# A two-layer decoder trunk on one core: x issued right behind the constants, the first layer's rows rounded out of PSUM, the rotation angles computed later

## The reference

```python
h = rms_norm(x, ln_mix_g[i])            # x * rsqrt(mean(x*x) + 1e-6) * g
proj = h @ w_in[i]                      # split into gates, conv, q_lat, kv_lat, k_rope, glu
q  = (rms_norm(q_lat,  q_norm_g)  @ w_uq)
kv = (rms_norm(kv_lat, kv_norm_g) @ w_ukv)
k_rope = apply_rope(k_rope_raw, cos, sin)   # cos, sin of positions * inv_freq
```

## Time and profile before

| | us |
|---|---|
| median of 3 runs | 1143.59 |
| lowest and highest of them | 1140.56, 1143.98 |
| span of the profiled execution | 1142.2 |
| TensorE busy in the span | 1090.8 |
| VectorE, ScalarE, GpSimd busy | 649.1, 356.2, 134.8 |

### The profile page before, as it was taken

How to read it: one execution, slowest core, us unless ns; L and a number is a source line. 1 busy time by engine, 2 the same in 40 slices (tenths; PEclk the granted TensorE clock), 3 DMA queues, 4 the chain that set the end, 5 groups by cost and what they waited for, 6 DMA issues and landing times. The chain is left out here.

```text
span 1142.2 us, 21367 instructions
## 1 busy us (share of the span) xinstructions
PE 1090.8 (95%) x8168; PEld 859.8 (75%) x8168; DVE 649.1 (57%) x1353; ACT 356.2 (31%) x600; POOL 134.8 (12%) x163
## 2 busy tenths in 40 slices
PE   5999999999899999999989999999999999999996
PEld 5988998998765555554889799999887555555566
DVE  6687997455543333333777879975437333333356
ACT  4355442233331111111663454423334111111143
POOL 0121320011000001000002032101101000000000
PEclk9999999999999999999999999999999999999998
DMA  7558974546279999999454778663644999999962
GB/s 205 131 158 257 304 228 147 151 145 204 111 275 407 416 417 417 418 418 385 135 148 135 224 248 240 200 184 113 179 134 168 400 417 417 417 418 418 417 219 95
DMA packets 202981, 300.39 MB, mean 263 GB/s; under 512 B 14000, under 2 KB 166544, under 8 KB 186512
## 3 DMA queue, kind: packets, MB, share of 16 engines
q1 hardware_dynamic: 202896, 299.28, 73.9%
HBM read 298.21 MB, written 1.05 MB: 262 GB/s over the span
## 5 line engine op out<-in xcount | busy, mean ns | idle before, releaser
L738 PE MATMUL ps<-h_pair,wsplit 128*128 128x256 f32 x2880 | 370.6, 289 | 16.0 <-DVE h_pair L1845 7.4
L738 PEld LDWEIGHTS ps<-h_pair,wsplit 128*128 128x128 f32 x2880 | 356.9, 194 | 24.3 <-issue 15.1
L1836 DVE TENSOR_TENSOR wsplit<-ring,wsplit 128x1024 fp32r<-128x1024 f32 x136 | 167.4, 1235 | 64.6 <-ACT wsplit L1295 60.7
L1295 ACT ACTIVATE wsplit<-ring 128x1024 fp32r<-128x1024 f32 x136 | 141.5, 1055 | 198.6 <-PE ps L738 116.8
L738 PE MATMUL ps<-gu_ring,hT 128*64 128x256 f32 x896 | 107.6, 383 | 3.1 <-DMA gu_ring<-in_w_exp_up_dram 3.1
L1958 DVE SCALAR_TENSOR_TENSOR work<-work,convT 128x256 f32<-128x256 f32 x240 | 104.7, 508 | 0.0
L1522 ACT ACTIVATE prow<-ps 128x128 f32<-128x128 f32 x64 | 17.7, 277 | 277.9 <-PE ps L738 277.9
L738 PEld LDWEIGHTS ps<-gu_ring,hT 128*64 128x64 f32 x896 | 61.7, 137 | 47.7 <-issue 14.0
L2249 DVE TENSOR_TENSOR hT_r<-ps,hT_r 128x512 fp32r<-128x512 f32 x64 | 44.3, 692 | 88.2 <-ACT hT_r L1295 88.2
L2234 DVE TENSOR_TENSOR prow<-prow,ps 128x128 f32<-128x128 f32 x64 | 18.4, 288 | 131.7 <-ACT prow L1522 131.7
L738 PE MATMUL ps<-work,ring 128*128 128x256 f32 x384 | 85.7, 379 | 0.0
(11 more groups left out here) (213 smaller groups left out, 1149.6 us busy)
## 6 DMA issues: line engine op xcount, KB each, us to landing
ring<-in_w_in_dram SPq DMA_DIRECT2D x104, 512.0 KB, 4.6
down_ring<-in_w_exp_down_dram SPq DMA_DIRECT2D x40, 1024.0 KB, 19.1
gu_ring<-in_w_exp_gate_dram SPq DMA_DIRECT2D x28, 1024.0 KB, 14.8
gu_ring<-in_w_exp_up_dram SPq DMA_DIRECT2D x28, 1024.0 KB, 17.0
lent_down<-in_w_exp_down_dram SPq DMA_DIRECT2D x24, 1024.0 KB, 19.6
gu_last<-in_w_exp_gate_dram SPq DMA_DIRECT2D x12, 1024.0 KB, 14.0
gu_last<-in_w_exp_up_dram SPq DMA_DIRECT2D x12, 1024.0 KB, 16.2
ring<-in_w_exp_gate_dram SPq DMA_DIRECT2D x12, 1024.0 KB, 14.9
```

The lines of the kernel that those rows point to most:

```text
L738: return nc.tensor.matmul(o, lhsT, rhs, start=first, stop=last)
L1295: return nc.scalar.activation(o, i, ACT.Copy)
L1836: TT(tile_split[:, m, 1, :, :], tile_of(name, m), tile_split[:, m, 0, :, :].bitcast(F32), ALU.subtract).then_inc(tile_low, 1)
```

## The change

- SyncE issues the constants, then x, then chunks `kv` and `q0` (four halves), then the positions, `w_kr` and the rest. The first layer's nine vector transfers are issued from ScalarE's queue. The positions now count on `kr_loaded`.
- ScalarE first runs a Sigmoid on one column, which loads that table.
- TensorE waits for constants and vectors, turns `vrow`, then x, then `crow`.
- ScalarE makes `h_high` straight from the PSUM banks, with g as scale (`first_high`, two operations a bank), and VectorE `h_low` from the same banks (`first_low`). The copies to `xT` (`first_x`) are all VectorE's and come after. Squares of x come after those copies. `hT`, needed only for the rotary key, is made by ScalarE as in the second layer.
- The first layer's kv is opened by `project_open` too. q0 waits until x is copied, since it uses one of its banks.
- The angles' first four steps come after q0 has been taken out of PSUM, the other six after the diagonal of kv. Sine and cosine come after the weights of q2, ahead of those of gg0.

```diff
@@ SyncE
-            sp.dma_start(ang[:, 0, :].bitcast(I32), positions[0].partition_broadcast(P)).then_inc(init_loaded, 16)
             sp.dma_start(cst[:, :], consts[:, :]).then_inc(init_loaded, 16)
+            sp.dma_start(xin, x[0].rearrange("(t q) d -> q t d", q=P)).then_inc(x_loaded, 16)
...
-            load_vectors(0)
-            sp.dma_start(xin, x[0].rearrange("(t q) d -> q t d", q=P)).then_inc(x_loaded, 16)
             for l in range(DEPTH):
                 load_chunk(l, CHUNKS[0])
+                load_chunk(l, CHUNKS[1])
                 if l == 0:
+                    sp.dma_start(ang[:, 0, :].bitcast(I32), positions[0].partition_broadcast(P)).then_inc(kr_loaded, 16)
                     load_rope_key(l)
@@ TensorE
-            pe.wait_ge(init_loaded, 32)
+            pe.wait_ge(init_loaded, 16)
+            pe.wait_ge(small_loaded, 16 * SMALL)
+            tr(ps[:, 7, 0:VROWS], vrow[:, :], VROWS).then_inc(vec_tr, 1)
             pe.wait_ge(x_loaded, 16)
...
+                project_open()
                 if l == 0:
-                    project_split("kv", "mix")
-                else:
-                    project_open()
+                    pe.wait_ge(x_in, 4)
                 project_split("q0", between=stat_of_x)
@@ ScalarE
+            load_vectors(act, 0)
+            act.wait_ge(const_set, 3)
+            nc.scalar.activation(last_act[:, :], mhalf[:, 0:1], ACT.Sigmoid)
+            def first_high(i):
+                act.wait_ge(x_tr, i + 1)
+                for c in (2 * i, 2 * i + 1):
+                    last = nc.scalar.activation(h_high[:, c, :], two(ps[:, i, :])[:, c % 2, :], ACT.Copy, scale=vcol("mix", c))
+                last.then_inc(rows_high[0], 1)
...
+                    first_high(0)
+                    high_tile(l, "kv", 0)
+                    first_high(1)
+                    high_tile(l, "kv", 1)
+                    first_high(2)
+                    first_high(3)
                     act.wait_ge(x_in, 4)
                     squares("mix", sq_x, xT, [None] * 4)
...
                 high_tiles(l, "q2")
+                if l == 0:
+                    act.wait_ge(rope_step, ROPE_STEPS)
+                    nc.scalar.activation(sinT[:, :], ang[:, 0, :], ACT.Sin).then_inc(rope_sin, 1)
+                    nc.scalar.activation(cosT[:, :], ang[:, 2, :], ACT.Sin).then_inc(rope_sin, 1)
                 high_tiles(l, "gg0")
@@ VectorE
+                def first_low(i):
+                    dve.wait_ge(rows_high[0], i + 1)
+                    for c in (2 * i, 2 * i + 1):
+                        last = STT(h_low[:, c, :], two(ps[:, i, :])[:, c % 2, :], vcol("mix", c), h_high[:, c, :].bitcast(F32), ALU.mult, ALU.subtract)
+                    last.then_inc(rows_low[0], 1)
+                def first_x(i):
+                    nc.vector.tensor_copy(xT[:, 2 * i:2 * i + 2, :], ps[:, i, :]).then_inc(x_in, 1)
...
                 take("q0", qn[:, 0:2, :])
+                if l == 0:
+                    angles()
                 low_tile(l, "q1", 1)
...
                 diagonal("kv")
+                if l == 0:
+                    reduced_angles()
                 scale_out("q2", qn[:, 4:6, :])
```

More of the change, by code:

```diff
@@ L516, in vcol, with load_vectors @@
             return vecT[:, VEC[name] + i:VEC[name] + i + 1]
+        def load_vectors(eng, l):
+            for name, w in (("mix", ln_mix_g), ("q", q_norm_g), ("kv", kv_norm_g), ("lng", ln_c_g),
+                            ("lnb", ln_c_b), ("ffn", ln_ffn_g), ("ple", ln_ple_g)):
+                n = w.shape[1] // P
+                eng.dma_start(vrow[VEC[name]:VEC[name] + n, :], w[l].rearrange("(c q) -> c q", q=P)).then_inc(small_loaded, 16)
+            eng.dma_start(vrow[VEC["ca"]:VEC["ca"] + KA * SCC, :], conv_a_w[l].rearrange("k (c q) -> (k c) q", q=P)).then_inc(small_loaded, 16)
+            eng.dma_start(crow[:, :], conv_c_w[l].rearrange("k (c q) -> (k c) q", q=P)).then_inc(small_loaded, 16)
         block = ctx.enter_context(nc.Block())
@@ L1302, in squares @@
                     nc.scalar.activation(dst[:, 2 * i:2 * i + 2, :], src[:, 2 * i:2 * i + 2, :], ACT.Square).then_inc(sq_ready[l], 1)
-            act.wait_ge(rope_step, ROPE_STEPS)
-            act.wait_ge(init_loaded, 32)
-            nc.scalar.activation(sinT[:, :], ang[:, 0, :], ACT.Sin).then_inc(rope_sin, 1)
-            nc.scalar.activation(cosT[:, :], ang[:, 2, :], ACT.Sin).then_inc(rope_sin, 1)
-            for i in range(2):
-                act.wait_ge(x_tr, 2 * i + 1)
-                copy(xT[:, 4 * i:4 * i + 2, :], ps[:, 2 * i, :]).then_inc(x_in, 1)
+            load_vectors(act, 0)
[6 more added lines that the diff above has]
+                last.then_inc(rows_high[0], 1)
             def high_tile(l, name, m):
@@ L1349, in _ @@
                 if l == 0:
-                    copy_vectors(0)
-                    high_tiles(l, "kv")
-                    high_rows(hT, [(h_ready[l], 2 * i + 2) for i in range(4)])
+                    act.wait_ge(vec_tr, 1)
+                    copy(vecT[:, :], ps[:, 7, 0:VROWS]).then_inc(vec_ready, 1)
+                    act.wait_ge(vec_ready, 1)
+                    first_high(0)
[4 more added lines that the diff above has]
+                    first_high(3)
                     act.wait_ge(x_in, 4)
                     squares("mix", sq_x, xT, [None] * 4)
+                    act.wait_ge(vec_tr, 2)
+                    copy(convT[:, :], ps[:, 6, 0:CROWS]).then_inc(vec_ready, 1)
                 def scaled_x(chunks):
-                    if l > 0:
-                        for c in chunks:
-                            nc.scalar.activation(hT[:, c, :], xT[:, c, :], ACT.Copy, scale=vcol("mix", c)).then_inc(h_ready[l], 1)
+                    for c in chunks:
+                        nc.scalar.activation(hT[:, c, :], xT[:, c, :], ACT.Copy, scale=vcol("mix", c)).then_inc(h_ready[l], 1)
                 high_tiles(l, "q0")
@@ L1872, in _ @@
                 if l == 0:
-                    low_rows(hT, "mix")
-                    low_tiles(l, "kv")
+                    dve.wait_ge(vec_ready, 1)
+                    first_low(0)
+                    first_low(1)
+                    low_tile(l, "kv", 0)
+                    first_low(2)
+                    low_tile(l, "kv", 1)
+                    first_low(3)
+                    for i in range(4):
+                        first_x(i)
                     add_square_pair(l, "mix", sq_x, 1)
@@ L1885, in _ @@
                 wait_unit(dve, l, "kv")
-                evacuates(l, TT(two(tmp[:, 0, :]), ps[:, 4:6, 0:S] if l else two(bank("kv")), bc2(), ALU.mult), "kv")
+                evacuates(l, TT(two(tmp[:, 0, :]), ps[:, 4:6, 0:S], bc2(), ALU.mult), "kv")
                 take("q0", qn[:, 0:2, :])
+                if l == 0:
+                    angles()
                 low_tile(l, "q1", 1)
```

51 lines of the change are left out of this document (19 added, 32 removed).

## The result

| | before | changed |
|---|---|---|
| median (range), runs | 1142.28 us (1140.56 to 1147.68), 22 | 1145.05 us (1143.04 to 1150.42), 22 |
| ratio to before, 95% interval | | 1.0023 [1.0014, 1.0032] |
| profiled execution / its span | 1144.0 / 1142.2 us | 1145.15 / 1143.3 us |

The changed kernel is 2.8 us, or 0.23%, slower by the medians. Its range ended at 1144.6, so both the time and the direction were missed. The 1144.0 in the table is inferred: an execution of the kernel before takes 1.7 to 1.9 us more than its span.

A forecast was written before the change was run, and what follows sets the result against it. TensorE, busy 95% of the span, was taken to bound the kernel. Gains of 2.2 (T) and 0.75 (to q0) less 0.2 (diagonal) and 0.95 (angles) gave 1.8 us, 1143.6 to 1141.8; range 1139.4 to 1144.6.

The forecast's parts named there:

- T: TensorE's first transpose of x, 10.10 us before: forecast at 7.9, 2.2 us earlier.
- The rival: Vectors on ScalarE's queue get through only after SyncE's transfers: T = 15, time 1148.5 us; chance 0.06.
- D: Distance from T to q0's second half, 18.95 us before: forecast 18.2, a gain of 0.75.
- E: Distance from q0's second half to the broadcast of q: forecast to lose 0.2 (diagonal) and 0.95 (angles).
- the lower bound: Earliest landing of x, constants and x at 402 GB/s: 7.1 us, making T 3.0 us earlier.
- the upper bound: Latest landing of x, constants again taking 4.6 us and x 2.6 more: 8.0 us.
- From T to q0: Chain of copies, squares and q0's first weight tile: q0's second half at T + 18.2, a gain of 0.75 us.
- kv's head start: kv starts 3.8 us sooner after T, of which 1.2 reaches q0, held by VectorE's copies and ScalarE's squares.
- The diagonal: Norm's diagonal behind q0's second half, late because VectorE makes q0's second low tile first: 0.2 us lost.
- The angles: Late angle steps and sines delay VectorE's taking of q2 and reach TensorE at q's diagonal: 0.95 us lost.
- The clock: Rival: idle time between kv and q0 halves TensorE's clock on q0's products, costing 1.7 us, 1143.5; chance 0.22.
- That the gain arrives at the end: A head start at q0 carries through mixer and experts to the end; rival that it is lost, 1143.6: chance 0.07.

The follow-up runs named there:

- the first profile: The changed kernel's first profiled execution, nothing further changed: 1145.15 us, its median over 22 runs 1145.05 us.
- the one with them spread: Changed kernel with vectors on SyncE behind x, ScalarE copying and squaring x bank by bank, angle steps in three places: 1138.75 us, ratio 0.9971.
- the repeat: The changed kernel run once more with not one line changed: 1146.88 us over 10 runs, ratio 1.0038.
- the filler: Changed kernel with TensorE multiplying constants (two unused products of 128x512) in its wait between kv and q0: 1142.72 us, ratio 1.0002.
- the last experiment: Kernel before with x right behind the constants, vectors behind x on SyncE, angles late, old copies kept: 1139.75 us, ratio 0.9983.
- the kernels with 4.6 and 5.4 us: Changed kernel with vectors on SyncE behind x and ScalarE's copies and squares interleaved: angle steps unspread 1139.91 us, spread 1138.75 us.

## Why the prediction was wrong

**T, the step that failed.** The prediction had the last vector issued at 3.5 and landed by 7.3, by the 3.8 us of the positions in the earlier trace rows, ahead of x. It was issued at 3.91, since ScalarE's first issue took 0.60 and others up to 0.40, and TensorE had it at 10.53, 6.6 us later. So T came 0.68 later where 2.2 earlier was forecast: 2.9 us wrong. The row of the positions was taken where almost nothing was in flight beside them, and what was in doubt was just how a small transfer fares beside 3.5 MB of SyncE's. The rival had this mechanism, and put it at T = 15, which was 4.2 us too late; its chance was 0.06. The measured 10.5 lies between these two ends, 7.3 and 15, and a range for T built from them would have held it. The forecast's own sum shows what this term does alone: with T at 10.78 it gives 0.7 + 0.4 = 1.1 us slower.

**What T explains.** Against the medians of 22 runs 1.8 us faster was forecast and 2.8 slower came, 4.6 apart. T is 2.9 of them. D and E together gained 0.1 where 0.4 was to be lost, which gives 0.5 back. The remaining 2.2 lie between the first profile's 0.56 and the medians. The number itself was missed by less, 3.3 us, by luck: the forecast stood on the median of three runs, 1143.6, which is 1.3 above that of 22. (The bounds that it names for its case add up to 1139.6 to 1143.4, not 1140.2 to 1143.2; that decides nothing.)

What pulled the chance down was a reading of the Trainium skill ("DMA: Bandwidth & Descriptors", "Queues, rings and completion order"): each DMA engine takes turns between the queues that have work. Nothing here contradicts that rule, but the conclusion did not follow. A turn is a whole packet of many descriptors, says the same section; the vectors made progress only slowly beside SyncE's queue (69 of 232 packets by 7.1 us, against 231 when the weights weren't there). Taking turns is no promise of being quick.

x itself did better than the value that I took: landed at 7.04, against 7.9, and the lower bound was 7.1. The constants took 3.5 us, not the 4.6 of the earlier trace rows, and the landing of x behind them 5.8. In the last experiment T is 6.96. Here a value next to the upper bound had been chosen, by the constants' row; the 4.6 of before had the positions' broadcast ahead of it. With the angles late alone, where just that broadcast was moved away, the constants took 3.2.

**From T to q0: right within 0.4 us.** Copies of x end at T + 10.9 (forecast 11.2), squares at T + 13.1 (13.4), q0's first product at T + 14.3 (14.6), idle time 1.60 (1 to 3), second half at T + 17.83 (18.2). The prices out of PSUM were 0.84 and 0.88 for a pair (0.91 and 0.88 taken). That a chain on other engines would let through only a third of kv's head start was the step that counted, and it held.

**The diagonal.** 0.2 was put down; the distance from q0's second half to q1's start is 3.41 against 3.32 before, so 0.1. VectorE had it written at 31.50, and TensorE was there at 31.57.

**The angles: right.** 0.95 forecast, E without the diagonal's 0.1 is 0.91 longer. The last of the ten steps ends by 46.1, the sines by 46.9, q2 is taken at 49.05, 0.55 later than before, or 0.99 later counted from q0's second half (0.97 forecast). The experiment with the steps back has E at 33.02, the one with them spread at 33.11.

**The clock: the rival that came on top.** It had 0.22 as an alternative to the forecast, at a price of 1.7, and the argument against it was that kv might itself run slow. Both happened, in different executions: kv slow and no fall (first profile), kv fast and a fall (the repeat). Over the profiles with a fall it cost 1.2 to 2.4 us on q0's products. As a rival it stood alone; but it needs only the idle time that the forecast itself contains, so it should have been a term of the sum with a chance of its own. At 62 us the change is 0.6 behind before without it and 2.8 with it. How much of the medians' 2.8 it makes is not shown: the filler brought back 2.3, with the doubts named there.

**That the gain arrives at the end** was assumed and given 0.07 against. The kernel before with x first shows it for 2.2 us; for the kernels with 4.6 and 5.4 us it arrives only in part by the medians, and why is open.

## What to carry to other kernels

When x is moved ahead, look for what else TensorE's first instruction waits for: moving some 90 KB to another engine's queue beside megabytes made it the last to land, at 10.5 us. Behind x on the same queue it was there at 8.1, still 1.4 after x; it cost nothing only where TensorE turned x first and the vectors after it. Ask of every gap on TensorE that an edit opens whether the clock survives it; fill it or close it, and forecast it as part of the edit, not as an accident. And take a change apart. Of its three parts one (x first) was worth 2 us and more. One (reads out of PSUM) shortened D by 1.1 us where the clock held and lengthened it by 0.2 to 1.1 where it fell; with copies and squares moved so that q0 stays behind kv it shortened D by 4, but the medians don't show that gain: 1139.9 with it and 1139.8 without, each 0.9983 of before beside it, with the angles late in both. One (angles late) cost 0.9 us, which another place gave back. And look behind the stretch that you edited, too: one profile there differed from another by up to 5.6 us.

## What the hardware showed that I had not expected

- A broadcast of one row of positions to 128 partitions, 128 KB, took 5.5 us and held the x behind it back by 2.0 us (7.8 against 5.8); queued ahead of the constants, in the kernel before, it cost these 1.0 to 1.4 us (4.6 against 3.2 to 3.6 in the kernels without).
- Nine transfers of 0.09 MB in all on ScalarE's queue took until 10.5 us beside SyncE's weights and until 7.9 without them.
- From the same program the clock rose at 20.2 us in one execution and at 13.6 in another, and kv's 44 products took 7.28 and 5.54 us. At 62 us the execution with the slower kv was 2.2 us ahead.
- From 62 us to the end, profiles differed by up to 5.6 us, with two to five stretches of granted clock 0.50 in them.
